# GpSimd's modulation products and sums in pieces of 512 columns

## What is computed

```python
cond = jax.nn.silu(c)
mod = (cond @ w_mod[i] + b_mod[i]).reshape(-1, N_SUBLAYERS, N_MOD, D_MODEL)

def _sublayer(x, fn, mod_j, g, b, weight):
    shift, scale, gate = mod_j[:, 0, None, :], mod_j[:, 1, None, :], mod_j[:, 2, None, :]
    y = fn(x * (1 + scale) + shift)
    return _layernorm(DEEPNORM_ALPHA * x + weight * gate * y, g, b)
```

## Time and profile before

| | us |
|---|---|
| median of 3 runs | 3169.07 |
| lowest, highest | 3165.86, 3175.72 |
| the profiled execution | 3178.11 |
| its span, first to last instruction | 3176.3 |
| GpSimd busy | 1093.7 |

### The profile page before, as it was taken

How to read it: one execution, slowest core, us unless ns; L and a number is a source line. 1 busy time by engine, 2 the same in 40 slices (tenths; PEclk the granted TensorE clock), 3 DMA queues, 4 the chain that set the end, 5 groups by cost and what they waited for, 6 DMA issues and landing times.

```text
span 3176.3 us, 52399 instructions
## 1 busy us (share of the span) xinstructions
PE 2771.4 (87%) x20695; PEld 2648.8 (83%) x20695; DVE 2217.4 (70%) x2628; ACT 1264.2 (40%) x1667; POOL 1093.7 (34%) x510
## 2 busy tenths in 40 slices
PE   3998699999985999999889999999779969779797
PEld 3998599999974999999864899999769969379797
DVE  6677877777768776786766677777877554774654
ACT  2434344344343443444332343443334434244443
POOL 0573635447183362472910057156460000000000
PEclk9998789999887898998975899899788989789898
DMA  8765556667471575774730376477454545034452
GB/s 301 246 239 152 182 173 237 222 217 252 149 272 57 186 264 179 237 256 154 259 120 0 115 244 250 166 248 249 132 175 146 185 155 173 27 105 135 132 179 86
DMA packets 357172, 576.21 MB, mean 181 GB/s; under 512 B 22255, under 2 KB 297898, under 8 KB 356906
## 3 DMA queue, kind: packets, MB, share of 16 engines
q1 hardware_dynamic: 357034, 574.29, 52.9%
HBM read 573.20 MB, written 1.05 MB: 181 GB/s over the span
## 4 chain that ended last, share of the span: by engine, by line
PE 65%; DVE 21%; issue 7%; ACT 3%; POOL 2%; DMA 1%; SPq 1%; DVEq 0%; POOLq 0%; ACTq 0%
PE ps L1547 59%; DVE wlo L1005 5%; ACT whi L648 2%; PE ps L1867 1%; DVE prob L1237 1%; DVE acc L1120 1%; PE ps L1858 1%; DVE acc L1036 1%; DVE z L1136 1%; DVE conv L1362 1%; POOL mod_w L630 1%; DVE std L1142 1%; POOL mod_acc L633 1%; DVE stat L1221 1%; PE ps L1715 1%
## 5 line engine op out<-in xcount | busy, mean ns | idle before, releaser
L1005 DVE TENSOR_TENSOR wlo<-raw,whi 128x1024 fp32r<-128x1024 f32 x804 | 1298.5, 1633 | 701.5 <-ACT whi L648 698.1
L648 ACT ACTIVATE whi<-raw 128x1024 fp32r<-128x1024 f32 x804 | 838.2, 1050 | 1235.7 <-PE ps L1547 1170.8
L1547 PE MATMUL ps<-H_hi,whi 128*128 128x256 f32 x4256 | 1227.8, 288 | 102.9 <-DVE H_lo L1154 37.6
L1547 PE MATMUL ps<-H_lo,whi 128*128 128x256 f32 x4256 | 1220.6, 287 | 0.0
L1547 PE MATMUL ps<-H_hi,wlo 128*128 128x256 f32 x4256 | 1219.8, 287 | 0.0
L1547 PEld LDWEIGHTS ps<-H_hi,whi 128*128 128x128 f32 x4256 | 834.8, 196 | 112.8 <-issue 80.2
L1547 PEld LDWEIGHTS ps<-H_lo,whi 128*128 128x128 f32 x4256 | 834.8, 196 | 0.1
L1547 PEld LDWEIGHTS ps<-H_hi,wlo 128*128 128x128 f32 x4256 | 833.8, 196 | 0.0
L633 POOL TENSOR_TENSOR mod_acc<-mod_acc,mod_w 128x1536 f32<-128x1536 f32 x154 | 614.6, 3991 | 25.2 <-POOL mod_w L630 25.2
L1547 PE MATMUL ps<-A_hi,whi 128*128 (+1 forms) x1880 | 540.2, 287 | 49.5 <-DVE wlo L1005 31.7
L624 POOL TENSOR_TENSOR pool_tick<-cond 128x1 f32<-128x1 f32 x176 | 135.2, 768 | 1255.0 <-DVE ax L1048 852.5
(11 more groups left out here) (276 smaller groups left out, 2239.1 us busy)
## 6 DMA issues: line engine op xcount, KB each, us to landing
raw<-in_ffn_w_in_dram SPq DMA_DIRECT2D x176, 1024.0 KB, 5.2
mod_w<-in_w_mod_dram SPq DMA_DIRECT2D x180, 768.0 KB, 6.3
raw<-in_ffn_w_out_dram SPq DMA_DIRECT2D x88, 1024.0 KB, 6.3
raw<-in_w_gate_up_dram SPq DMA_DIRECT2D x22, 1024.0 KB, 5.1
raw<-in_ssm_w_in_dram SPq DMA_DIRECT2D x20, 1024.0 KB, 6.9
raw<-in_w_in_dram SPq DMA_DIRECT2D x14, 1024.0 KB, 5.0
raw<-in_diff_w_in_dram SPq DMA_DIRECT2D x12, 1024.0 KB, 7.2
raw<-in_w_down_dram SPq DMA_DIRECT2D x11, 1024.0 KB, 4.9
```

The lines of the kernel that those rows point to most:

```text
L648: return nc.scalar.activation(dst, src, ACT.Copy)
L1005: tt(wlo[b % 2][:, r], raw[b % RAW][:, r], whi[b % 2][:, r].bitcast(F32), ALU.subtract).then_inc(w_lo, 1)
L1547: m = pe.matmul(out, l, r, start=first and i == 0, stop=last and i == 2, skip_group_check=rest)
```

## The change

In GpSimd's loop the product of a unit is issued as three instructions of 512 columns, and so is the sum; the k = 0 product too. Each piece of a product raises `pool_step` by one, and each piece of a sum waits for its own piece of the product. `mod_used` is still raised once a unit, by the last piece. Loads, buffers, `pool_tick` and all other engines' instructions are as before.

```diff
+PIECE = 512
...
-                            w = mod_w[:, half, :]
+                            w, total = mod_w[:, half, :], mod_acc[:, half, :]
+                            pieces = [slice(i, i + PIECE) for i in range(0, MODU, PIECE)]
                             if k == 0:
-                                nc.gpsimd.tensor_scalar(mod_acc[:, half, :], w, cond[:, 0:1], 1.0, ALU.mult, ALU.mult)\
-                                    .then_inc(mod_used, 1)
+                                for i, r in enumerate(pieces):
+                                    first = nc.gpsimd.tensor_scalar(total[:, r], w[:, r], cond[:, 0:1], 1.0, ALU.mult, ALU.mult)
+                                first.then_inc(mod_used, 1)
                                 continue
-                            nc.gpsimd.tensor_scalar(w, w, cond[:, k:k + 1], 1.0, ALU.mult, ALU.mult).then_inc(pool_step, 1)
-                            pool.wait_ge(pool_step, sub * 14 - 14 + 2 * (k - 1) + half + 1)
+                            for r in pieces:
+                                nc.gpsimd.tensor_scalar(w[:, r], w[:, r], cond[:, k:k + 1], 1.0, ALU.mult, ALU.mult).then_inc(pool_step, 1)
+                            done = len(pieces) * (2 * (k - 1) + half)
                             pool.wait_ge(mod_used, sub * 16 + 2 * k + half - 1)
-                            nc.gpsimd.tensor_tensor(mod_acc[:, half, :], mod_acc[:, half, :], w, ALU.add)\
-                                .then_inc(mod_used, 1)
+                            for i, r in enumerate(pieces):
+                                pool.wait_ge(pool_step, (sub - 1) * 14 * len(pieces) + done + i + 1)
+                                added = nc.gpsimd.tensor_tensor(total[:, r], total[:, r], w[:, r], ALU.add)
+                            added.then_inc(mod_used, 1)
```

## The result

Four runs of the changed kernel have a median of 3140.3 us (3136.38 to 3141.86), beside 3172.39 us (3165.86 to 3180.16) for the kernel before on the same chip: a ratio of 0.9891, with a 95% interval of 0.987 to 0.9913. The forecast was 3124, its range 3080 to 3160. The profiled execution lasted 3138.9 us (span 3137.1), against 3178.1 (3176.3) before. The profiled spans differ by 39.2 us and the medians by 32.1; the profiled execution of before lies 9 above the median that was known when the prediction was made (3169.1, of three runs; a fourth moved it to 3172.4).

The account below looks back on a forecast made before the run. GpSimd and VectorE shut each other out of shared ports for whole instructions, stalling TensorE in places. FFN -30, MLA -22, diff attention -5, projections +12 give -45 us: 3124 on the median's scale, range 3080 to 3160 (own range 3095 to 3150).

Parts of the forecast that it names:

- Rival B: Whole kernel: gain stays in the FFN, MLA waits for sums, projections for loads; -20 us, 3149 us; chance 0.20.
- C: Whole kernel: nearly all contention goes, no fixed part per piece; -75 us, 3094 us; chance 0.13.
- D: Whole kernel: nothing moves, many small waits replace few long ones on the same path; 3169 us; chance 0.10.
- E: Whole kernel slower: GpSimd doesn't let go between pieces, VectorE waits for them all; about +45 us, 3214 us; chance 0.07.
- FFN, -30: Seven FFNs with GpSimd at work: shorter VectorE waits remove TensorE stalls, 30 of 34.5 us gained, not less than 15.
- GpSimd's price, 0.5 a unit: GpSimd's modulation unit: four more instructions lengthen a clean unit by 0.5 us, from 5.30 to 5.8.
- SSM, +8: SSM, twelve units: slower GpSimd and VectorE's round with pieces coming between lose 8 us.
- diff projection, +4: Diff attention's projection: eight units at GpSimd's pace, each 0.5 us longer, lose 4 us through loads queued behind sums.
- two kinds of unit: SSM: GpSimd slower by 0.5 us in five units; in seven VectorE's round may gain 0.8 from a piece between.
- MLA, -22: Two MLA layers: shorter VectorE waits would gain 16 us a layer, limited to 10 and about 12, together 22.
- the cap: MLA's end: GpSimd ends when it did, so its slack of 10 us (14 in the first layer) limits the gain.
- L1005 "at most about 2.5 us long": VectorE's low-part subtraction: expected sign, longest about 2.5 us, mean down from 1.63 toward 1.35.

## Why the prediction was right, point by point

**Forecast against rivals.** The measured 3140 lies 16 above the forecast, and inside its own range of 3095 to 3150. Of the forecast 45 us, 39 came between the profiled executions and 32 between the medians. The shape was that of the forecast: the gain is in the FFNs *and* in MLA, and the projections pay. Rival B kept MLA's gain at nothing (measured: 16.7); C and D are far off. E is refuted as a whole, and yet it happens (below). Both signs by which I would be wrong did show, though each in one place or a few: TensorE waits 6.45 us for GpSimd at the end of the first MLA (B's sign), and VectorE was kept out over boundaries four times (E's). The heads of MLA are also not under 4.2 us apart, as I had said.

**FFN, -30, measured -32.5.** The size was right and each of its signs is there. One step was incomplete. I had written that a stall comes when a 3.5 us wait meets a slack of 2.3, as if the length of the sum alone decided. The kernel with extra instructions ahead of the product has sums at least as long and loses only 6 us of the 32: the phase decides which of VectorE's subtractions the sum meets, and the price hangs on that. What pieces do is make the FFN indifferent to the phase: 208.8 to 209.5 us in each of the six after the first, where the two kernels with extra instructions spread from 209.2 to 213.0.

**GpSimd's price, 0.5 a unit, measured 0.6.** One clean unit in the timeline of GpSimd (first MLA):

```profile
361.23 0.19 POOL L625 TENSOR_TENSOR pool_tick<-cond 128x1 f32<-128x1 f32 x1
361.39 2.02 POOL L634 TENSOR_SCALAR mod_w<-mod_w,cond 128x512 f32<-128x512 f32 x3
363.38 3.75 POOL L639 TENSOR_TENSOR mod_acc<-mod_acc,mod_w 128x512 f32<-128x512 f32 x3
367.10 0.19 POOL L625 TENSOR_TENSOR pool_tick<-cond 128x1 f32<-128x1 f32 x1
```

367.10 - 361.23 = 5.87 us, against 5.30. The three pieces of a product take 2.02 where the whole one took 1.57, those of a sum 3.75 where the whole one took 3.46, and the 0.16 between is gone. The upper bound, the one-column instruction, was nearly the value. The estimate worked out from the Trainium skill (GPSIMD Engine Reference, section Elementwise — side-by-side cycle accounting), 0.1 a unit, was far too low: the trace has 0.57.

**SSM, +8, measured +7.5; diff projection, +4, measured +6.5.** A unit of the SSM projection, in GpSimd's timeline:

```profile
1530.14 0.19 POOL L625 TENSOR_TENSOR pool_tick<-cond 128x1 f32<-128x1 f32 x1
1530.31 4.04 POOL L634 TENSOR_SCALAR mod_w<-mod_w,cond 128x512 f32<-128x512 f32 x3
1534.31 3.80 POOL L639 TENSOR_TENSOR mod_acc<-mod_acc,mod_w 128x512 f32<-128x512 f32 x3
1538.08 0.19 POOL L625 TENSOR_TENSOR pool_tick<-cond 128x1 f32<-128x1 f32 x1
```

and SP's queue beside it:

```profile
1530.20 0.34 SPq L546 DMA_DIRECT2D mod_w<-in_w_mod_dram  x1
...
1538.14 0.34 SPq L546 DMA_DIRECT2D mod_w<-in_w_mod_dram  x1
1538.53 0.43 SPq L537 DMA_DIRECT2D raw<-in_ssm_w_in_dram  x1
```

1538.08 - 1530.14 = 7.94 us, against 7.26, and in the same microsecond SP issues the slice and only then the block. Twelve units of some 0.6 are the 7.5 us. My mechanism of two kinds of unit (five of 0.5, seven of 0.8) gave the same sum without being needed. The spaced queue shows that the load queue behind GpSimd's sums held the stage up, by 7 us with whole sums and with cut ones; that pieces cost 5 us even with that queue spaced (331.4 against 326.2) was in no term of mine. In diff attention I had counted eight units of 0.5; 6.5 us is eight of 0.8. With whole instructions there the stage gets 2.3 us back, not 6.5, so pieces help its heads and hurt its projection, as forecast (-5 and +4, measured -4.9 and +6.5).

**MLA, -22, measured -16.7: the mis-sized term.** In three parts, each read between the starts of VectorE's first instruction of the first head, of the last head, and of the centring in the next layer norm:

| us, first and second MLA | before | after | moved | forecast |
|---|---|---|---|---|
| before attention | 84.8, 85.8 | 79.1, 80.9 | -5.7, -4.9 | -8, -8 |
| first head to last head | 32.1, 28.6 | 24.6, 25.9 | -7.5, -2.7 | -8, -8 |
| behind the last head, with the wait for GpSimd | 36.9, 38.3 | 40.8, 38.5 | +3.9, +0.2 | +4, +6 |

What set the length in both is the cap, and it was the cap that I had mis-sized. VectorE's first instruction of the layer norm shows what the stage had gained before TensorE's wait for the sums (first MLA before and after, then the second):

```profile
412.03 0.88 DVE L1127 SCALAR_TENSOR_TENSOR z<-ps,gw,ax 128x256 f32<-128x256 f32 x2 [4.76 <-PE ps L1547]
391.25 0.88 DVE L1133 SCALAR_TENSOR_TENSOR z<-ps,gw,ax 128x256 f32<-128x256 f32 x2 [4.75 <-PE ps L1553]
...
2378.26 0.88 DVE L1127 SCALAR_TENSOR_TENSOR z<-ps,gw,ax 128x256 f32<-128x256 f32 x2 [2.98 <-PE ps L1547]
2335.60 0.88 DVE L1133 SCALAR_TENSOR_TENSOR z<-ps,gw,ax 128x256 f32<-128x256 f32 x2 [4.66 <-PE ps L1553]
```

Counted from the stage's start, they come 146.6 and 130.4 us in, and 145.5 and 135.1: 16.2 us sooner in the first MLA, where the forecast had 16, and 10.4 in the second. (In the first, 3.0 of the 16.2 came behind the last head, where I had counted nothing; so the match is in part luck.) Of these, 6.9 and 3.1 were lost again behind it, with TensorE's waits of 6.45 and 2.49 us for GpSimd. Two things in the cap were wrong. The slack was measured to the layer norm's first matmul at 2384.66, but TensorE needs the sums at 2382.31, when it adds them up:

```profile
416.08 1.17 PE L1617 MATMUL ps<-K,mod_acc 128*128 128x1 f32 x10
...
2382.31 1.17 PE L1617 MATMUL ps<-K,mod_acc 128*128 128x1 f32 x10
```

GpSimd's last sums end at 403.9 and 2374.2 us, so the slack was 12.2 us in the first MLA and 8.1 in the second, not 14 and 10. And GpSimd's end didn't stay where it was: its last sum ends 141.0 us behind the stage's start in the first MLA, where it ended at 138.5, and 141.7 in the second, where it ended at 141.4. 12.2 less 2.5 and 8.1 less 0.3 leave 9.7 and 7.8; measured are 9.3 and 7.4. One more step failed, without showing in the total: I had taken the first layer's heads for the second, where the eight heads had only 28.6 us and gave 2.7. With the cap where it was, more from the heads would have become a longer wait.

The heads in VectorE's timeline (their first instruction, and the normalisation):

```profile
351.04 0.54 DVE L1224 TENSOR_TENSOR prob<-ps,K 128x384 f32<-128x384 f32 x1
353.02 2.47 DVE L1243 TENSOR_SCALAR prob<-prob,stat 128x128 f32<-128x128 f32 x2
355.75 0.54 DVE L1224 TENSOR_TENSOR prob<-ps,K 128x384 f32<-128x384 f32 x1
...
360.40 0.54 DVE L1224 TENSOR_TENSOR prob<-ps,K 128x384 f32<-128x384 f32 x1
362.21 1.36 DVE L1243 TENSOR_SCALAR prob<-prob,stat 128x128 f32<-128x128 f32 x2
364.51 0.56 DVE L1224 TENSOR_TENSOR prob<-ps,K 128x384 f32<-128x384 f32 x1 [0.28 <-PE ps L1694]
```

They come 4.7, 4.7 and 4.1 us apart, against 5.35 and the 3.8 I worked out. The normalisation waits up to 1.9 us (2.47 for 0.55), where I took 0.5 as the mean. A likely reason is that 0.5 is the mean for a request that comes at any moment, while VectorE asks again as soon as it is served, and so meets the start of the next piece more often; no run tested it.

**L1005 "at most about 2.5 us long": wrong.** Its mean fell as said (1.63 to 1.42, short of 1.35), but the longest is 4.84 us. This is it, in VectorE's timeline and then GpSimd's:

```profile
892.64 5.98 DVE L1011 TENSOR_TENSOR wlo<-raw,whi 128x1024 fp32r<-128x1024 f32 x2 [6.99 <-ACT whi L654]
```

```profile
892.66 3.72 POOL L639 TENSOR_TENSOR mod_acc<-mod_acc,mod_w 128x512 f32<-128x512 f32 x3
```

Three pieces of a sum run through in 3.72 us, as long as undisturbed, while VectorE's subtraction, which had begun 0.02 us before the first, waits for all three. That is rival E, over two boundaries. The same pair stands at 1500.77 and 1500.82 (5.98 and 3.71 us). Two more subtractions, of 4.42 and 4.75 us at 916.68 and 2322.29, began 0.4 and 0.2 us behind the first piece and waited for the rest of all three. The other 800 take at most 2.32 us, and the four lie outside the FFNs, which is why E's 45 us didn't come. With pieces of 256 columns it happens more often: the subtraction of 7.90 us, at 374.86, waits for six pieces of a product and then six of a sum (their rows in GpSimd's timeline):

```profile
374.75 2.77 POOL L634 TENSOR_SCALAR mod_w<-mod_w,cond 128x256 f32<-128x256 f32 x6
377.46 4.22 POOL L639 TENSOR_TENSOR mod_acc<-mod_acc,mod_w 128x256 f32<-128x256 f32 x6
```

With only the sums cut the longest is 2.57 us, the limit that I had forecast. What decides at a boundary who goes first stays open: no run varied it alone.

## What to carry to other kernels

Where two engines shut each other out for whole instructions, cutting the long ones on the engine with room pays only as far as the other engine's wait reaches the end. Try to cut the longest kind alone (here the sums, not the products), and count each cut as a fixed price wherever that engine sets a pace, be it through a load queue or at a stage's end. Before crediting such a gain to length, shift the long instruction by half a microsecond with a few tiny ones: if the time falls, the phase has a part in it. When a forecast rests on slack, measure the slack to the instruction that waits, not to a later one. And look at what is queued behind the slower engine, since three edited lines of the load queue gave 7 us in the SSM with whole sums and with cut ones.

## What the runs showed of the hardware that I had not expected

- A GpSimd instruction of a single column takes 0.16 to 0.19 us, and cutting a long one costs nearly as much for each further piece: 0.14 us by the clean unit (0.57 and four more instructions), 0.18 with the gap of 0.16 that went.
- VectorE can be passed over at a boundary between two GpSimd instructions. With pieces of 512 columns in sum and product four of its 804 subtractions waited for the end of three pieces of a sum (the longest: 4.84 us, of which 1.2 are its own). Two had started at most 0.05 us ahead of the first piece, two up to 0.4 us behind it. With pieces of 256 columns 20 took over 4 us, up to 7.90, and with only the sums in 512 none over 2.57.
- Four one-column instructions, 0.62 us of added work for each unit, made the kernel 0.7% faster (0.9926), by moving a long sum past the start of a subtraction; the same four behind the sum gave 0.2%.
- Of the three ways of cutting, one is no gain at all: pieces of 512 columns in sum and product 0.9891, of 256 columns 1.0025, the sums alone in 512 0.9855.
